# The last block's gate pieces leave on SyncE's queue instead of ScalarE's, spread over the end of one stage and the start of the next

## The chip, the cores and the metric

The kernel runs on one core of one Trainium2 chip, as one launch. The metric is device time in microseconds, the median of several executions.

## The reference

One inference step of a two-layer backbone over 384 tokens (128 of context, 256 latent). Each layer mixes tokens (short convolution, pooling, attention) and then mixes channels with a product-key expert retrieval over 16,384 experts. The change lies in that second half, which is by far the longer one:

```python
def _peer(x, w_q, sub_keys, u, v):          # D = 1024, 8 heads, 128 keys, top 16
    q = (xt @ w_q).reshape(T, PEER_HEADS, 2, PEER_HALF)
    s = jnp.einsum('thpd,hpkd->thpk', q, sub_keys)
    sv, si = lax.top_k(s, PEER_TOPK)
    cand = sv[:, :, 0, :, None] + sv[:, :, 1, None, :]
    top, f = lax.top_k(cand, PEER_TOPK)
    experts = i1 * PEER_KEYS + i2                      # i1, i2 looked up through f
    gates = jax.nn.softmax(top, axis=-1)
    h = jax.nn.gelu(jnp.einsum('tkd,td->tk', u[ec], xc))
    return jnp.einsum('tk,tkd->td', gc * h, v[ec])
```

## The kernel before

The kernel does not gather experts for most tokens. For 352 of the 384 tokens it computes the retrieval densely, in two stages per layer. The other 32 tokens (the "sparse" ones, the last of the third token block) go through gathered rows of `u` and `v`.

**The first stage** makes the hidden activations. It has 128 units, one for each block of 128 experts (`hidden_step`, L941 to L952 on TensorE). A unit is 24 matmuls: eight slices of `D`, and for each three products (`h_lo*u_hi`, `h_hi*u_hi`, `h_hi*u_lo`), since a 32-bit number is split in a high and a low part. ScalarE makes the high part of the weights (`u_hi`, L1229) and VectorE the low part (`u_lo`, L1642), both for the unit after next's buffer, so TensorE's unit 121 can't start before ScalarE and VectorE have treated its weights. ScalarE also applies the gelu to each finished unit (`act_h`, L1222, L1245) into a ring of four buffers, from which SyncE stores it to `act_scratch` in device memory (L510). Each gelu waits for the store of four units before.

**The gates.** Beside the first stage the routing of the three token blocks runs on VectorE. For a dense block the gates then have to be laid out over all experts: 16 gate steps scatter them into `g_all`, a tile of 128 keys x 128 tokens per partition. A block's `g_all` goes out to `gate_scratch` in eight pieces of 16 keys, 1024 KB each, in rows of 128 tokens (512 bytes). One semaphore for each piece (`g_st[0]` to `g_st[7]`) counts its landing. The two dense blocks are number 1 and 2 of the order. Block 1's pieces go out on SyncE's queue, one at a time between other things (`store_gates`, L495 to L499, called in L523). Block 2, the last, has its gates complete after unit 119 of the stage. Its eight pieces are issued by ScalarE in a row at L1291 to L1295, ahead of the gelu of unit 119 (`last_gelu`, L1245) and of the weights of unit 121. Eight units are left then: 120 to 127.

**The second stage** multiplies by `v`. It has 256 units of 12 matmuls (L1011), in groups of eight: a group is four blocks of 128 experts in two halves of the output. ScalarE and VectorE split the weights again (`v_hi` L1304, `v_lo` L1859; each instruction serves two units), and once per four units VectorE multiplies activation and gate (`w` from `act`, `gate`, L1868), with `w_hi` (L1311) and `w_lo` (L1872) behind it. Each of these engines works through one fixed order: in step 8(g-1) VectorE multiplies the first `w` of group g, and behind it in the row stands the `v_lo` of the pair of units 8(g-1)+2.

SyncE's queue brings in the data, each step waiting for the release of a buffer:

- `wring`, four slots of 1024 KB: `u` for the first stage, `v` for the second (`load_v`, L550), one slot per half group.
- `gate2` and `act2`, two buffers of a group each: `load_ga` (L543 to L547), 704 KB of gates and 704 KB of activations. Group 4 and later are loaded in a hardware loop (L592) that runs from group 4 to 31.
- Before the loop SyncE waits for all of `g_st[3:]` and `act_st` (L586 to L591).

GpSimd waits for every `g_st` and for the last unit of the first stage before it writes into the space of `g_all`: it makes `sel` (L712), then in the first layer loads `c_b` and `mod_w` (L719, L622; 1024 KB each) for the next layer's modulation, and in both layers fetches rows of `v` for the sparse tokens (L617). ScalarE needs `c_b` at step 22 of the second stage (L1339), VectorE the first two rows at step 24 (L1881).

Of the kernel before, what the change touches and what calls it, by code (L numbers as in the profile page):

```python
# [16 lines left out]
P = 128  # L17
# [5 lines left out]
TB = T // P  # L23
# [42 lines left out]
WR = 4  # L66
AR = 4
# [11 lines left out]
GT = TB - SCATTERED  # L79
# [3 lines left out]
ORDER = (2, 0, 1)  # L83
# [15 lines left out]
PIECES = 8  # L99
# [28 lines left out]
def build(nc, x_t, c_t, c_rows, vecs_t, w_ada, w_mod, w_in, w_out, w_q, subkeys_t, u_t, v_t, u_rows, v_rows, bias_t, pool_t, ck_t, cv_t, consts,  # L128
# [87 lines left out]
    g_all = at("g_all", [P, NK, P])  # L216
# [40 lines left out]
    gate_dram = nc.dram_tensor("gate_scratch", (NK, P, T), F32).ap()  # L257
# [7 lines left out]
    def S(name, per, credit=0):  # L265
        return Signal(nc, ctx, name, per, credit)
# [81 lines left out]
    tq_evac = S("tq_evac", NQ, credit=2)  # L348
    g_st = [S(f"g_st{i}", 16 * GT, credit=16) for i in range(PIECES)]
# [16 lines left out]
    sc_st = S("sc_st", 16 * PH * TOPK)  # L366

    uhi_rdy = S("uhi_rdy", NB)
    ulo_rdy = S("ulo_rdy", NB)
    h_mm = S("h_mm", NB, credit=2)  # L370
    gelu_rdy = S("gelu_rdy", NB, credit=2)
    act_st = [S(f"act_st{i}", 16 * (NB // AR), credit=16) for i in range(AR)]
# [27 lines left out]
    sp_passed = S("sp_passed", 0)  # L400
# [63 lines left out]
    def _(sp):  # L464
# [8 lines left out]
        for l in range(DEPTH):  # L473
# [31 lines left out]
            def store_acts(i, s):  # L505

                sp.wait_ge(gelu_rdy.sem, gelu_rdy.at(l, 0) + (i * (2 * WR) + 2 * (s - WR)))
                for b in range(2):
                    p = 2 * ((s + 1) % 2) + b
                    sp.dma_start(act_dram[i * (2 * WR) + (2 * (s - WR - 1) + b), :, 0:TD], act_h[:, p, 0:TD]) \  # L510
                      .then_inc(act_st[p].sem, 16)
# [22 lines left out]
            for turn in range(3, NB // 8):  # L534
                tb = max((b for b in range(SCATTERED, TB) if GATES_END[b] < turn), default=None)
# [7 lines left out]
            def load_ga(g, buf):  # L543

                for dst, src in ((gate2, gate_dram), (act2, act_dram)):
                    sp.dma_start(dst[:, buf, :, 0:TD], src[bass.ds(g * G, G), :, 0:TD].rearrange("b e t -> e b t")) \
                      .then_inc(ga_ld[buf].sem, 16)  # L547

            def load_v(g, half, slot):
                sp.dma_start(wring[:, slot].rearrange("p k n -> p (k n)"), v_t[l, g, half]).then_inc(w_ld[slot].sem, 16)  # L550

            for n in range(WR + 1):

                if n < WR:
                    sp.wait_ge(ulo_rdy.sem, ulo_rdy.at(l, NB + 2 * (n + 1 - WR)))
                    load_v(n // 2, n % 2, n)
                if n:
                    store_acts(NB // (2 * WR), n)
                if n == 1:
                    for sig in g_st[:2]:  # L560
                        sp.wait_ge(sig.sem, sig.at(l, 16 * GT))
                        sp.sem_inc(sp_passed.sem, 1)
                    for sig in act_st:
                        sp.wait_ge(sig.sem, sig.at(l, 16 * (4 * G // AR)))
                        sp.sem_inc(sp_passed.sem, 1)
                    sp.wait_ge(sc_st.sem, sc_st.at(l, 16 * PH * TOPK))
                    sp.sem_inc(sp_passed.sem, 1)
                    load_ga(0, 0)
                    sp.wait_ge(g_st[2].sem, g_st[2].at(l, 16 * GT))
                    sp.sem_inc(sp_passed.sem, 1)  # L570
                    load_ga(1, 1)
            def group_loads(g, n, ga=True):

                if ga:
                    sp.wait_ge(w32_rdy.sem, l * NB + (g - 1) * G)
                    load_ga(g, n)
                for half in range(2):
                    slot = 2 * n + half

                    sp.wait_ge(vlo_rdy.sem, l * NV + (g * (2 * G) + (G * (half - 3) + vlo_rdy.credit)))  # L580
                    load_v(g, half, slot)

            for n in range(2):
                group_loads(2 + n, n)
            for sig in g_st[3:]:
                sp.wait_ge(sig.sem, sig.at(l, 16 * GT))  # L586
                sp.sem_inc(sp_passed.sem, 1)
# [448 lines left out]
    def _(act):  # L1036
# [63 lines left out]
        for l in range(DEPTH):  # L1100
# [46 lines left out]
            for n in range(NU + 2):  # L1147
# [8 lines left out]
                if n < NU:  # L1156
                    keys = P if unit(n)[1] == 0 else KEYS
# [89 lines left out]
            for tb in range(TB):  # L1247
# [23 lines left out]
                for g in range(GATE_STEPS):  # L1271
# [5 lines left out]
                    for k in range(4):  # L1277
                        t = 8 * g + 4 + k
# [7 lines left out]
                                   ps[:, 0].rearrange("p (t i) -> p i t", t=4)).then_inc(gq_evac.sem, 1)  # L1286
                    act.wait_ge(tq_mm.sem, Q + (1 + tq_mm.credit))
                    nc.scalar.copy(g_all[:, :, 8 * g + 4:8 * g + 8], two_halves(g)[:, 0]).then_inc(half_rdy.sem, 1)
                if tb + 1 == TB:
                    act.wait_ge(tq_evac.sem, tq_evac.at(l, NQ))  # L1290
                    act.wait_ge(gq_evac.sem, gq_evac.at(l, NQ))  # L1291
                    for piece in range(PIECES):
                        keys = slice(piece * (NK // PIECES), (piece + 1) * (NK // PIECES))
                        act.dma_start(gate_dram[keys, :, ORDER[tb] * P:(ORDER[tb] + 1) * P].rearrange("a b t -> b a t"), g_all[:, keys]) \  # L1294
                            .then_inc(g_st[piece].sem, 16)  # L1295
                last_gelu(GATES_END[tb])
            def v_hi_step(i, n, lap=0):

# [735 lines left out]
```

## Time and profile before

| | |
|---|---|
| time, median of 3 runs | 2777.58 us (2775.84 to 2782.12) |
| the profiled execution | 2781.91 us, its span 2780.1 us |
| TensorE matmul busy | 2652.0 us, 95% of the span |
| VectorE | 1975.0 us, 71% |
| ScalarE | 1216.4 us, 44% |
| GpSimd | 681.6 us, 25% |
| chain that ended last | TensorE 77%, VectorE 11%, issue 4%, DMA 3%, ScalarE 2%, ScalarE's DMA issues 2% |
| DMA | 632.86 MB, 228 GB/s over the span |
| SyncE's queue (q1), ScalarE's queue (q10) | 500.51 MB and 16.78 MB |

The span is what the instructions cover; the execution's own time is 1.8 us more. TensorE is busy almost throughout, so what matters are the few places where it is not. "ACTq" and "SPq" are the two sequencers while they issue a DMA; such time doesn't count as busy. ScalarE's queue carries nothing but the sixteen pieces (eight in each layer).

### The profile page before, as it was taken

Reading aid. Unit: us, or ns where it says so; the run is one execution under the profiler, and the core shown is the slowest. Engines: PE = TensorE matmul, PEld = TensorE weight load, DVE = VectorE, ACT = ScalarE, POOL = GpSimd, SP = SyncE. Lnnn points to the kernel's source line nnn. Section 1 sums busy time; section 2 is a strip of 40 time slices with the busy share of each in tenths; the row PEclk is TensorE's granted clock in tenths of the full one; section 3 lists DMA queues with packets and bytes.
Section 4 is the critical chain, followed back from the end, with each engine's and each line's share of the span. In section 5 each row is a group of like instructions: output and inputs, shape, how many; then the busy total and the mean of one; then the engine's idle time right before and its main releaser. Section 6 shows DMA issues by size and latency. Waiting matters only on the chain.

```text
span 2780.1 us, 44944 instructions
## 1 busy us (share of the span) xinstructions
PE 2652.0 (95%) x16866; PEld 2592.2 (93%) x16866; DVE 1975.0 (71%) x3668; ACT 1216.4 (44%) x2061; POOL 681.6 (25%) x493
## 2 busy tenths in 40 slices
PE   7999999999996999999999899999999789999998
PEld 6979999899996999999998899998999789999998
DVE  3536686998893688888765567789988645666664
ACT  3444543366473433333354454334745533333333
POOL 0011008777600111111111000477764000101010
PEclk8999999999998999999999899999999999999999
DMA  7383359757948889898645124896596587777771
GB/s 299 125 313 132 132 190 347 224 154 191 257 132 268 322 312 345 315 341 324 245 155 159 61 107 168 293 280 179 143 259 188 173 285 280 257 277 266 268 265 73
DMA packets 274517, 632.86 MB, mean 228 GB/s; under 512 B 43888, under 2 KB 208112, under 8 KB 229296
## 3 DMA queue, kind: packets, MB, share of 16 engines
q1 hardware_dynamic: 185856, 500.51, 51.8%
q0 software_dynamic: 55472, 113.44, 13.4%
q10 hardware_dynamic: 33024, 16.78, 2.1%
q8 instruction: 95, 1.56, 0.2%
q14 instruction: 70, 0.57, 0.1%
HBM read 535.59 MB, written 94.99 MB: 227 GB/s over the span
## 4 chain that ended last, share of the span: by engine, by line
PE 77%; DVE 11%; issue 4%; DMA 3%; ACT 2%; ACTq 2%; POOL 1%; SPq 0%; POOLq 0%; DVEq 0%
PE ps L1011 33%; PE ps L952 23%; PE ps L806 11%; DVE u_lo L1642 3%; PE ps L828 2%; PE ps L976 2%; ACTq L1294 2%; DMA act_scratch<-act_h 2%; PE ps L913 1%; PE ps L982 1%; PE ps L935 1%; PE ps L902 1%; DVE u_rows_s L1654 1%; PE ps L881 1%; DVE best_iu L1734 1%
## 5 line engine op out<-in xcount | busy, mean ns | idle before, releaser
L952 PE MATMUL ps<-h_lo,u_hi 128*128 128x352 f32 x2048 | 668.6, 326 | 70.5 <-DVE u_lo L1642 69.4
L1011 PE MATMUL ps<-w_hi,v_lo 128*128 128x352 f32 (+1 forms) x2048 | 661.9, 323 | 5.3 <-DVE v_lo L1859 5.1
L1011 PE MATMUL ps<-w_hi,v_hi 128*128 128x352 f32 x2048 | 664.6, 324 | 0.0
L952 PE MATMUL ps<-h_hi,u_hi 128*128 128x352 f32 x2048 | 663.4, 324 | 0.0
L952 PE MATMUL ps<-h_hi,u_lo 128*128 128x352 f32 x2048 | 662.3, 323 | 0.0
L1011 PE MATMUL ps<-w_lo,v_hi 128*128 128x352 f32 x2048 | 659.7, 322 | 0.0
L1304 ACT CAST v_hi<-wring 128x1024 fp32r<-128x1024 f32 x256 | 268.5, 1049 | 607.8 <-PE ps L1011 607.8
L1859 DVE TENSOR_TENSOR v_lo<-wring,v_hi 128x1024 fp32r<-128x1024 f32 x256 | 313.4, 1224 | 282.5 <-ACT v_hi L1304 282.5
L703 POOL DMA_INDIRECT gate_scratch<-scat_g,scat_i x256 | 435.6, 1701 | 151.2 <-issue 105.4
L952 PEld LDWEIGHTS ps<-h_lo,u_hi 128*128 128x128 f32 x2048 | 386.6, 189 | 84.1 <-DVE u_lo L1642 82.7
L1642 DVE TENSOR_TENSOR u_lo<-wring,u_hi 128x1024 fp32r<-128x1024 f32 x256 | 312.7, 1222 | 202.7 <-ACT u_hi L1229 199.9
L1011 PEld LDWEIGHTS ps<-w_hi,v_lo 128*128 128x128 f32 x2048 | 383.9, 187 | 6.5 <-DVE v_lo L1859 6.5
L1011 PEld LDWEIGHTS ps<-w_lo,v_hi 128*128 128x128 f32 x2048 | 388.7, 190 | 0.0
L952 PEld LDWEIGHTS ps<-h_hi,u_lo 128*128 128x128 f32 x2048 | 387.4, 189 | 0.0
L952 PEld LDWEIGHTS ps<-h_hi,u_hi 128*128 128x128 f32 x2048 | 386.8, 189 | 0.0
L1011 PEld LDWEIGHTS ps<-w_hi,v_hi 128*128 128x128 f32 x2048 | 384.9, 188 | 0.0
L1222 ACT ACTIVATE act_h<-ps 128x352 f32<-128x352 f32 x250 | 117.2, 469 | 458.9 <-PE ps L952 404.9
L1229 ACT CAST u_hi<-wring 128x1024 fp32r<-128x1024 f32 x256 | 267.1, 1043 | 0.0
L617 POOL DMA_INDIRECT v_rows_s<-in_v_rows_dram,pick_s x64 | 88.0, 1375 | 556.2 <-PE ps L1011 546.1
L806 PE MATMUL ps<-g_lo,u_hi 128*128 128x386 f32 x576 | 198.6, 345 | 6.6 <-DVE g_lo L1417 5.6
L806 PE MATMUL ps<-g_hi,u_lo 128*128 128x386 f32 x576 | 196.3, 341 | 0.0
L806 PE MATMUL ps<-g_hi,u_hi 128*128 128x386 f32 x576 | 196.0, 340 | 0.0
(267 smaller groups left out, 3444.9 us busy)
## 6 DMA issues: line engine op xcount, KB each, us to landing
wring<-in_u_t_dram SPq DMA_DIRECT2D x128, 1024.0 KB, 5.6
wring<-in_v_t_dram SPq DMA_DIRECT2D x128, 1024.0 KB, 5.5
act_scratch<-act_h SPq DMA_DIRECT2D x256, 176.0 KB, 5.9
gate<-gate_scratch SPq DMA_DIRECT2D x64, 704.0 KB, 6.5
act<-act_scratch SPq DMA_DIRECT2D x64, 704.0 KB, 8.5
wring<-in_w_ada_dram SPq DMA_DIRECT2D x24, 1024.0 KB, 6.3
mod_w<-in_w_mod_dram POOLq DMA_DIRECT2D x24, 1024.0 KB, 7.4
wring<-in_w_in_dram SPq DMA_DIRECT2D x20, 1024.0 KB, 4.8
```

The costliest lines, as they stand in the source:

```text
L617: pool.indirect_dma_start(v_rows_s[:, s % V_RING], None, v_rows, bass.IndirectOffsetOnAxis(ap=pick_s[:, 0, s:s + 1].bitcast(U32), axis=0)) \
L703: pool.indirect_dma_start(gate_cells, bass.IndirectOffsetOnAxis(ap=scat_i[0:P - NS, j:j + 1], axis=0), scat_g[0:P - NS, j:j + 1], None, co ...
L806: last = nc.tensor.matmul(ps[:, bank, 0:TS], w[:, M % 2, k], gx[:, k, 0:TS], start=(k == 0 and n == 0), stop=(k == KC - 1 and n == 2))
L828: last = nc.tensor.matmul(ps[:, m % 2, 0:T], w[:, m % 2, k], hx[:, k, 0:T], start=(k == 0 and n == 0), stop=(k == KC - 1 and n == 2))
L952: last = nc.tensor.matmul(ps[:, 6 + s % 2, 0:TD], u[:, s % 2, k], hx[:, k, 0:TD], start=(k == 0 and n == 0), stop=(k == KC - 1 and n == 2))
L976: last = nc.tensor.matmul(ps[:, 0, k * P:(k + 1) * P], one_a[:, k], one_b[:, k], start=True, stop=True)
L1011: last = nc.tensor.matmul(ps[:, half * (KC // 2) + c, cols], v[:, of % 4, d], w[:, group * G + of, cols], start=(opening and k == 0), stop ...
L1222: nc.scalar.activation(act_h[:, p, 0:TD], ps[:, 6 + p % 2, 0:TD], ACT.Gelu_apprx_tanh) \
L1229: nc.scalar.copy(u_hi[:, b].rearrange("p k e -> p (k e)"), wring[:, slot].rearrange("p k n -> p (k n)")[:, b * D:(b + 1) * D]) \
L1304: nc.scalar.copy(v_hi[:, n % 4:n % 4 + 2].rearrange("p a n -> p (a n)"), wring[:, tile].rearrange("p k n -> p (k n)") [:, (n % G) * 512:(n ...
L1642: V.tensor_tensor(u_lo[:, b].rearrange("p k e -> p (k e)"), wring[:, slot].rearrange("p k n -> p (k n)")[:, b * D:(b + 1) * D], u_hi[:, b] ...
L1859: V.tensor_tensor(v_lo[:, n % 4:n % 4 + 2].rearrange("p a n -> p (a n)"), wring[:, n // G].rearrange("p k n -> p (k n)") [:, (n % G) * 512 ...
```

## The change

ScalarE's loop over the eight pieces of the last block goes, with its two waits. SyncE issues the pieces instead: piece 0 as soon as the gates are complete, pieces 1 and 2 each behind a load of `v` and two stores of activations, still in the first stage; pieces 3 and 4 behind the loads for group 2 and pieces 5, 6 and 7 behind those for group 3, in the second stage. The loop over `n` is written out as `first_v` calls, the two `load_ga` before the stage stand farther apart, and the waits ahead of them come in another order. The wait for `g_st[3:]` before the hardware loop and GpSimd's wait for all `g_st` stay as they are.

```diff
-            for n in range(WR + 1):
-                if n < WR:
-                    sp.wait_ge(ulo_rdy.sem, ulo_rdy.at(l, NB + 2 * (n + 1 - WR)))
-                    load_v(n // 2, n % 2, n)
-                if n:
-                    store_acts(NB // (2 * WR), n)
-                if n == 1:
...
-                    load_ga(0, 0)
-                    sp.wait_ge(g_st[2].sem, g_st[2].at(l, 16 * GT))
-                    sp.sem_inc(sp_passed.sem, 1)
-                    load_ga(1, 1)
+            def first_v(n):
+                sp.wait_ge(ulo_rdy.sem, ulo_rdy.at(l, NB + 2 * (n + 1 - WR)))
+                load_v(n // 2, n % 2, n)
+
+            gates_made(TB - 1)
+            store_gates(TB - 1, 0)
+            first_v(0)
+            store_acts(NB // (2 * WR), 1)
+            store_gates(TB - 1, 1)
+            first_v(1)
+            store_acts(NB // (2 * WR), 2)
+            store_gates(TB - 1, 2)
...
+            load_ga(0, 0)
+            first_v(2)
+            store_acts(NB // (2 * WR), 3)
+            sp.wait_ge(g_st[2].sem, g_st[2].at(l, 16 * GT))
+            sp.sem_inc(sp_passed.sem, 1)
+            load_ga(1, 1)
+            first_v(3)
+            store_acts(NB // (2 * WR), 4)
...
             for n in range(2):
                 group_loads(2 + n, n)
+                for piece in ((3, 4), (5, 6, 7))[n]:
+                    store_gates(TB - 1, piece)
             for sig in g_st[3:]:
                 sp.wait_ge(sig.sem, sig.at(l, 16 * GT))
...
-                if tb + 1 == TB:
-                    act.wait_ge(tq_evac.sem, tq_evac.at(l, NQ))
-                    act.wait_ge(gq_evac.sem, gq_evac.at(l, NQ))
-                    for piece in range(PIECES):
...
-                        act.dma_start(gate_dram[keys, :, ORDER[tb] * P:(ORDER[tb] + 1) * P].rearrange("a b t -> b a t"), g_all[:, keys]) \
-                            .then_inc(g_st[piece].sem, 16)
                 last_gelu(GATES_END[tb])
```

ScalarE's row at the end of the last gate step, first layer, before the change (line numbers of the kernel before):

```order
L1285 COPY g_all<-ps 128x128x4
L1288 COPY g_all<-ps 128x128x4
L1294 DMA gate_scratch<-g_all 128x16x128 x8
L1245 ACTIVATE act_h<-ps 128x352
L1229 CAST u_hi<-wring 128x1024
L1222 ACTIVATE act_h<-ps 128x352
```

And with the change, in which the same lines stand twelve lines lower:

```order
L1297 COPY g_all<-ps 128x128x4
L1300 COPY g_all<-ps 128x128x4
L1257 ACTIVATE act_h<-ps 128x352
L1241 CAST u_hi<-wring 128x1024
L1234 ACTIVATE act_h<-ps 128x352
```

The eight transfers are gone from the row, and the gelu of unit 119 follows the last copy directly.

SyncE's row from the last stores of the loop over `u` to the end of group 1's loads, first layer, before:

```order
L510 DMA act_scratch<-act_h 128x352 x4
L550 DMA wring<-in_v_t_dram 128x2048 x2
L510 DMA act_scratch<-act_h 128x352 x2
L546 DMA gate_120<-gate_scratch 128x4x352
L546 DMA act_121<-act_scratch 128x4x352
L546 DMA gate_120<-gate_scratch 128x4x352
L546 DMA act_121<-act_scratch 128x4x352
L550 DMA wring<-in_v_t_dram 128x2048
L510 DMA act_scratch<-act_h 128x352 x2
L550 DMA wring<-in_v_t_dram 128x2048
L510 DMA act_scratch<-act_h 128x352 x4
```

With the change, up to the load of group 1:

```order
L510 DMA act_scratch<-act_h 128x352 x4
L498 DMA gate_scratch<-g_all 128x16x128
L550 DMA wring<-in_v_t_dram 128x2048
L510 DMA act_scratch<-act_h 128x352 x2
L498 DMA gate_scratch<-g_all 128x16x128
L550 DMA wring<-in_v_t_dram 128x2048
L510 DMA act_scratch<-act_h 128x352 x2
L498 DMA gate_scratch<-g_all 128x16x128
L546 DMA gate_120<-gate_scratch 128x4x352
L546 DMA act_121<-act_scratch 128x4x352
L550 DMA wring<-in_v_t_dram 128x2048
L510 DMA act_scratch<-act_h 128x352 x2
```

Three pieces now stand between the loads of `v` and the stores, and group 1's pair comes behind the third load of `v`.

SyncE's row from group 2's loads to the branch into the hardware loop, with the change:

```order
L546 DMA gate_120<-gate_scratch 128x4x352
L546 DMA act_121<-act_scratch 128x4x352
L550 DMA wring<-in_v_t_dram 128x2048 x2
L498 DMA gate_scratch<-g_all 128x16x128 x2
L546 DMA gate_120<-gate_scratch 128x4x352
L546 DMA act_121<-act_scratch 128x4x352
L550 DMA wring<-in_v_t_dram 128x2048 x2
L498 DMA gate_scratch<-g_all 128x16x128 x3
L604 UNCONDITIONAL_BRANCH
```

Before, the same row held neither of the two L498 entries.

## Rows read from the trace of the kernel before

**Rows 1.** The waits, summed over the span: in total, times, longest.

```profile
DVE u_lo L1642 <- ACT u_hi L1229: 199.9, 97, 26.1
```

**Rows 2.** Chain that ended last, 780 to 1100 us: start, duration, what.

```profile
848.33 1.90 ACTq L1294
850.25 3.63 ACTq L1294
...
868.70 3.66 ACTq L1294
872.82 1.04 ACT u_hi L1229
```

**Rows 3.** Timeline of TensorE: start, duration, line, what, idle time before it.

```profile
850.00 0.32 PE L952 MATMUL ps<-h_hi,u_lo 128*128 128x352 f32 x1
875.17 0.66 PE L952 MATMUL ps<-h_lo,u_hi 128*128 128x352 f32 x1 [24.85 <-DVE u_lo L1642]
...
903.98 0.34 PE L1011 MATMUL ps<-w_hi,v_lo 128*128 128x384 f32 x1
...
2232.99 0.66 PE L952 MATMUL ps<-h_lo,u_hi 128*128 128x352 f32 x1 [24.80 <-DVE u_lo L1642]
```

**Rows 4.** Timeline of ScalarE after the pieces, first and second layer.

```profile
880.98 0.47 ACT L1222 ACTIVATE act_h<-ps 128x352 f32<-128x352 f32 x1 [5.82 <-PE ps L952]
...
884.84 0.47 ACT L1222 ACTIVATE act_h<-ps 128x352 f32<-128x352 f32 x1 [2.46 <-PE ps L952]
...
949.62 1.92 ACT L1339 ACTIVATE c_b<-c_b 128x2048 f32<-128x2048 f32 x1
...
2239.11 0.46 ACT L1222 ACTIVATE act_h<-ps 128x352 f32<-128x352 f32 x1 [6.13 <-PE ps L952]
```

**Rows 5.** Pieces by line, SyncE's then ScalarE's: issue in ns, landing in us.

```profile
L498 SPq DMA_DIRECT2D gate_scratch<-g_all x16: 382/383/383, 673.1 to 2101.8; - x16
DMA to landing us min/median/max: 6.0/6.8/8.1
...
DMA to landing us min/median/max: 5.2/10.3/13.7
```

**Rows 6.** Timeline of VectorE around the start of the second stage.

```profile
900.23 0.83 DVE L1868 TENSOR_TENSOR w<-act,gate 128x704 f32<-128x704 f32 x1
...
906.09 0.89 DVE L1868 TENSOR_TENSOR w<-act,gate 128x704 f32<-128x704 f32 x1 [0.24 <-DVE w_lo L1872]
906.90 1.22 DVE L1859 TENSOR_TENSOR v_lo<-wring,v_hi 128x1024 fp32r<-128x1024 f32 x1
...
920.93 0.89 DVE L1868 TENSOR_TENSOR w<-act,gate 128x704 f32<-128x704 f32 x1 [2.23 <-DMA act<-act_scratch]
```

**Rows 7.** Landing of L546's pairs issued at 884-889, 905-907 and 2289-2292 us.

```profile
DMA to landing us min/median/max: 6.5/8.6/10.5
...
DMA to landing us min/median/max: 12.8/13.5/14.3
...
DMA to landing us min/median/max: 6.7/8.2/9.6
```

**Rows 8.** Timeline of SyncE in the second stage: issues for groups 3 and 4.

```profile
915.21 0.45 SPq L546 DMA_DIRECT2D gate<-gate_scratch  x1
...
922.99 7.68 SPq L550 DMA_DIRECT2D wring<-in_v_t_dram  x2
931.70 0.40 SPq L546 DMA_DIRECT2D gate<-gate_scratch  x1
```

**Rows 9.** One stretch of the second stage: busy times, granted clock, DMA share, GB/s.

```profile
908.20:923.70 15.50, 15.50 (x96) 15.50 (x97) 8.76 (x9) 5.62 (x6) 0.00 (x0) 1.00 1.01 396
```

**Rows 10.** Timeline of GpSimd after the first stage, and the landing of its first load.

```profile
904.32 0.25 POOL L712 TENSOR_TENSOR sel<-cst 128x32 f32<-128x32 f32 x1 [143.87 <-PE ps L952]
...
905.90 0.62 POOL L719 DMA_DIRECT2D c_b<-in_c_rows_dram  x1
```

```profile
c_b<-in_c_rows_dram POOLq DMA_DIRECT2D x1, 1024.0 KB, 6.5
```

More of the change, by code:

```diff
@@ L550, in load_v @@
                 sp.dma_start(wring[:, slot].rearrange("p k n -> p (k n)"), v_t[l, g, half]).then_inc(w_ld[slot].sem, 16)
-            for n in range(WR + 1):
-                if n < WR:
-                    sp.wait_ge(ulo_rdy.sem, ulo_rdy.at(l, NB + 2 * (n + 1 - WR)))
-                    load_v(n // 2, n % 2, n)
-                if n:
-                    store_acts(NB // (2 * WR), n)
-                if n == 1:
-                    for sig in g_st[:2]:
-                        sp.wait_ge(sig.sem, sig.at(l, 16 * GT))
-                        sp.sem_inc(sp_passed.sem, 1)
[L563 to L567, printed above, removed]
-                    load_ga(0, 0)
-                    sp.wait_ge(g_st[2].sem, g_st[2].at(l, 16 * GT))
-                    sp.sem_inc(sp_passed.sem, 1)
-                    load_ga(1, 1)
+            def first_v(n):
[9 more added lines that the diff above has]
+            store_gates(TB - 1, 2)
+            for sig in act_st:
+                sp.wait_ge(sig.sem, sig.at(l, 16 * (4 * G // AR)))
+                sp.sem_inc(sp_passed.sem, 1)
+            sp.wait_ge(sc_st.sem, sc_st.at(l, 16 * PH * TOPK))
+            sp.sem_inc(sp_passed.sem, 1)
+            for sig in g_st[:2]:
+                sp.wait_ge(sig.sem, sig.at(l, 16 * GT))
+                sp.sem_inc(sp_passed.sem, 1)
+            load_ga(0, 0)
+            first_v(2)
+            store_acts(NB // (2 * WR), 3)
+            sp.wait_ge(g_st[2].sem, g_st[2].at(l, 16 * GT))
+            sp.sem_inc(sp_passed.sem, 1)
+            load_ga(1, 1)
+            first_v(3)
+            store_acts(NB // (2 * WR), 4)
             def group_loads(g, n, ga=True):
@@ L1288, in _ @@
                     nc.scalar.copy(g_all[:, :, 8 * g + 4:8 * g + 8], two_halves(g)[:, 0]).then_inc(half_rdy.sem, 1)
-                if tb + 1 == TB:
-                    act.wait_ge(tq_evac.sem, tq_evac.at(l, NQ))
-                    act.wait_ge(gq_evac.sem, gq_evac.at(l, NQ))
-                    for piece in range(PIECES):
-                        keys = slice(piece * (NK // PIECES), (piece + 1) * (NK // PIECES))
-                        act.dma_start(gate_dram[keys, :, ORDER[tb] * P:(ORDER[tb] + 1) * P].rearrange("a b t -> b a t"), g_all[:, keys]) \
-                            .then_inc(g_st[piece].sem, 16)
                 last_gelu(GATES_END[tb])
```

## The prediction

> **What bounds the kernel now.** I read the page first (TensorE is busy 95% of the span), then the waits. Their row to look at is that of `u_lo`, which waits for ScalarE 97 times with a longest of 26.1 us [rows 1], far out of line with a usual wait of a microsecond or two. The chain of waits around the longest one shows where it comes from: ScalarE's sequencer issues the eight gate pieces, the second in 1.90 us and each later one in about 3.66, and only then makes the `u_hi` of unit 121 at 872.82 [rows 2]. TensorE's timeline gives the price: its last matmul of unit 120 starts at 850.00, the first of unit 121 at 875.17, after 24.85 us of idleness; in the second layer it is 24.80 [rows 3]. So the pieces are on the path that sets the end, twice.
>
> There is a second, smaller price. Unit 121's first matmul lasts 0.66 us where the one before the stall lasts 0.32 [rows 3], and the whole unit is slow: its gelu starts at 880.98, 5.8 us after the unit's start, while the next comes 3.86 us later [rows 4]. That is 1.9 us; in the second layer 2239.11 less 2232.99 is 6.1 us, so 2.2 us [rows 3, 4].
>
> **What goes.** With the loop gone ScalarE passes from the last copy to the gelu of unit 119 and the weights of unit 121, which are ready before unit 120 ends at 850.3, as in all gate steps ahead of it. Gain: 24.85 + 1.9 + 24.80 + 2.2 = 53.8 us. Everything in the first stage's tail then stands 26.8 us earlier: the first matmul of the second stage, which I call S, moves from 903.98 [rows 3] to 877.2. Nothing of this gain needs the issue to be cheap on SyncE, only that nobody on the path waits for SyncE. That is the rest of the sum.
>
> **What an issue costs on SyncE.** Block 1's sixteen pieces, issued there with other things between, take 0.38 us each and land after 6.0 to 8.1 us; ScalarE's, in a row, land after 10.3 in the median [rows 5]. The first is the price of the issue, and 3.66 us is the rate at which 1024 KB of 512-byte rows drain, once two pieces are under way [rows 2]. Here the Trainium skill speaks against the change ("DMA: Bandwidth & Descriptors", section "Issuing engines are not separate DMA queues"): spreading DMAs over engines saves only the sequencer's time to initiate them, usually small beside the DMA. By that rule, with 0.38 us a piece, sixteen pieces would free some 6 us of ScalarE; the trace disagrees, since a piece held ScalarE for 3.66 us. But its other half, that all share the same sixteen engines, holds: the 3.66 us of draining go along to SyncE's queue.
>
> **The tail, 850 to 877.** Piece 0 goes out at about 849, piece 1 at 855.7 (behind the gelu of unit 121 and its stores), piece 2 at 863.3, each alone, so SyncE isn't held. Group 0's pair goes out right behind piece 2, at 863.8, since pieces 0 and 1 have landed. It drains behind piece 2 and should take the 10.5 us of [rows 7]: 874.3, against 900.23 - 26.8 = 873.4, when VectorE is ready for the first `w` [rows 6]. Group 1's pair must wait for piece 2 (863.3 + 6.8 or 10.3) and for the stores of units 124 and 125 at 870.1: it goes out at 871 to 873.6 and lands at 877.5 to 884, against 906.09 - 26.8 = 879.3 [rows 6]. Behind that `w` stands the `v_lo` of units 2 and 3; it ended at 908.12 and TensorE needed it at 903.98 + 3.87 = 907.85 [rows 3, 6], so there is no slack, and lateness is paid in full. Cost per layer 0 to 5 us; I take 1.8, nearest to a pair landing at 881. The stores of activations keep their place in time: a gelu needs the store of four units before, issued some 11 us earlier against a landing of about 6.
>
> **The start of the second stage.** The times count from S. A unit lasts 1.93 us (half of 3.86 us for half the matmuls). VectorE multiplies group g's first `w` in step 8(g-1) and must have made the `v_lo` behind it by unit 8(g-1)+2. That needs the pair landed by S + 15.46(g-1) + 3.87 - 0.82 - 1.22 = S + 15.46(g-1) + 1.8. (Group 2 before: limit S + 17.3 = 921.3, landed 920.93 [rows 6]: no harm.)
>
> Group 3's pair went out at S + 11.2 [rows 8]; now pieces 3 and 4 are ahead of it, and it drains from S + 20.9: load of `v` from 10.9 at 396 GB/s [rows 9], 2.7 us, then 2 x 3.66. Its 1.44 MB take 3.6 us more, landing by about S + 27; limit S + 32.7. No cost.
>
> Group 4 is the place to look at. Before, its pair went out at S + 27.7, limit S + 48.2. Now pieces 5 to 7 go out behind the second load of `v` for group 3, at S + 26.7 (922.99 + 7.68, [rows 8]), and SyncE then waits for them to land. The queue before them is empty at about S + 29.9 (the pair to 24.5, two loads of `v` 2.7 each); three pieces add 11.0: drained at 40.9, landed at 43.3. The loop takes 1.0 us to start (930.67 to 931.70 [rows 8]), so the pair goes out at S + 44.3, and lands 6.9 to 9.6 us later as in the quiet case: S + 51.2 to 53.9, 3.0 to 5.7 us past the limit [rows 7]. I take 4 us for the second layer.
>
> In the first layer GpSimd, too, waits for all pieces. It came to `sel` at 904.32 and to `c_b` 1.6 us later [rows 10]; now it does at S + 43.3 and 45.1, so its 3 MB for the modulation fall on the late pair. Before, that collision made group 2's pair land after 14.3 us [rows 7]: S + 58.6, a stall of 10.4. By ScalarE: `c_b` lands after 6.5 us [rows 10], S + 51.6, its silu takes 1.92 [rows 4], and `v_hi` and `v_lo` of unit 26 (1.05 and 1.22) end near S + 56 where TensorE needs them at S + 50.2: some 6 to 7 us. The two run side by side; I take 9 between them (5 to 14). GpSimd's rows for the sparse tokens are late by as much, and hidden in the same stall.
>
> The skill's page on DMA (section "Queues, rings and completion order") says that each engine takes turns between queue rows, but serves one row in order. In the old kernel a load of `v` could pass between ScalarE's pieces; now it stands behind them. My sums for groups 3 and 4 go by that; by taking turns group 3's pair would land 7.3 us sooner, and nothing else changes.
>
> **The sum.** -53.8 + 2 x 1.8 + 4 + 9 = -37.2 us. The profiled execution (span 2780.1, own time 2781.9) would take 2744.7. It is 4.3 us above the median of the runs, so the median comes to 2740.4. Loops and all later groups find their loads in time as before: after group 4 SyncE is again a group ahead.
>
> **The rivals.**
> *All of it arrives.* Stalls in the tail and at group 4 are absorbed (the pieces drain at more than 286 GB/s, the pair lands in 5 us). For it: pairs have landed in 6.7 us. Against it: GpSimd's loads can't move ahead of the pieces. Gain over 48 us, up to 53.8: 2724 to 2730. Chance 0.13.
> *Back-pressure in the tail.* The sum of the tail's traffic (3 pieces, 4 loads of `v`, 2 pairs, the stores) is 3 x 3.66 + 4 x 2.7 + 2 x 3.6 and some 5 for the stores, 34 us in 27. If the stores of activations fall behind it, the gelu waits for its buffer, and with it `u_hi`. A landing of 13.7 us as with the slowest piece [rows 5] instead of the 11 allowed costs 2.7 at each of two or three pairs of units, in each layer 5 to 8 us: 2750 to 2765 in all. Chance 0.13.
> *Slower.* The place is SyncE's wait for pieces 3 to 7 ahead of the hardware loop. If the three last ones don't share one drain but land 13.7 us each one after the other, it ends at S + 26.7 + 41.1 = 67.8, and group 4's pair lands at S + 83 (14.3 us), 35 us late in each layer: -53.8 + 3.6 + 70 = +20, 2797. It decides the sign once the wait ends later than about S + 60. For it: DMA share 1.01 in this stretch [rows 9]. Against it: eight pieces in a row landed after 10.3 us each while overlapping. Chance 0.03.
> *It does not do what it says.* TensorE's idleness stays, since unit 121 waited for something else that came at the same time. Against it: `u_hi` starts the moment ScalarE is free [rows 2]. Within 6 us of before: chance 0.02.
>
> **How the numbers follow.** The forecast has 0.69: its own range is -20 to -48, 2730 to 2757. Of the rivals' 0.31, the fast end and most of the back-pressure case should be inside: 2727 to 2760. About 0.2% (5.6 us) is what a measurement can tell from no change: faster 0.95, same 0.02, slower 0.03.
>
> **What would show it.** The issues of pieces at 0.38 us on SyncE, and no wait of `u_lo` over 7 us in the first stage. Unit 121 right behind unit 120. In the tail, `w` waiting for the pairs of group 0 or 1 by 1 to 3 us. In the second stage TensorE waits near S + 50 for `v_lo`, 4 us in the second layer and more than that in the first, with DMA or `c_b` behind it; groups 2, 3 and 5 without a wait. The prediction is wrong if the stall near S + 50 is missing or over 15 us, or if gelus wait for stores in the tail.

## The result, and the profile after

| | before | after |
|---|---|---|
| median | 2779.85 us (4 runs) | 2751.11 us (4 runs, 2745.57 to 2755.03) |
| ratio to before | | 0.9894, 95% interval 0.9869 to 0.9919 |
| the profiled execution | 2781.91 us | 2745.57 us (span 2743.7) |
| TensorE waits for `u_lo` in the first stage | 69.4 us | 19.7 us |
| TensorE waits for `v_lo` in the second stage | 5.1 us | 25.6 us |

The change makes the kernel 28.7 us faster by the medians; 37 were forecast, a little more than the 23 to 36 us that the interval allows. From part 5 of the page before, the two groups of matmuls that start a unit:

```profile
L952 PE MATMUL ps<-h_lo,u_hi 128*128 128x352 f32 x2048 | 668.6, 326 | 70.5 <-DVE u_lo L1642 69.4
L1011 PE MATMUL ps<-w_hi,v_lo 128*128 128x352 f32 (+1 forms) x2048 | 661.9, 323 | 5.3 <-DVE v_lo L1859 5.1
```

Parts 4 and 5 of the page after:

```profile
PE 77%; DVE 11%; DMA 5%; issue 4%; ACT 2%; SPq 1%; POOL 0%; POOLq 0%; ACTq 0%; DVEq 0%
...
L1023 PE MATMUL ps<-w_hi,v_lo 128*128 128x352 f32 (+1 forms) x2048 | 665.8, 325 | 26.6 <-DVE v_lo L1864 25.6
L964 PE MATMUL ps<-h_lo,u_hi 128*128 128x352 f32 x2048 | 666.3, 325 | 21.0 <-DVE u_lo L1647 19.7
```

ScalarE's issues have left the chain, DMA has grown in it, and the idle time before TensorE has moved from the stage of `u` to the stage of `v`. (Lines stand twelve or five lower than before: L1241 is the cast to `u_hi`, L1234 and L1257 the gelu, L1023 the second stage's matmul, L1864 `v_lo`, L1873 the product `w`.)

**The stop that was to go is gone.** Before, on ScalarE's timeline in the first layer, 25.35 us lay between the last copy (846.52) and the gelu of unit 119:

```profile
847.87 24.49 ACTq L1294 DMA_DIRECT2D gate_scratch<-g_all  x8
872.46 0.46 ACT L1245 ACTIVATE act_h<-ps 128x352 f32<-128x352 f32 x1 [25.35 <-issue]
```

After, the gelu of unit 119 and `u_hi` of unit 121 follow the last copy, and the gelus of units 120 and 121 come at the usual distance of 3.84 us:

```profile
846.67 0.48 ACT L1257 ACTIVATE act_h<-ps 128x352 f32<-128x352 f32 x1
847.02 1.05 ACT L1241 CAST u_hi<-wring 128x1024 fp32r<-128x1024 f32 x1
850.02 0.46 ACT L1234 ACTIVATE act_h<-ps 128x352 f32<-128x352 f32 x1 [1.95 <-PE ps L964]
850.38 1.03 ACT L1241 CAST u_hi<-wring 128x1024 fp32r<-128x1024 f32 x1
853.86 0.46 ACT L1234 ACTIVATE act_h<-ps 128x352 f32<-128x352 f32 x1 [2.44 <-PE ps L964]
```

**What came instead.** All stops of TensorE of over 0.25 us in this part of the program, from its timeline; the first four in the first layer, the last four in the second. They answer to [rows 3].

```profile
877.66 0.41 PE L1023 MATMUL ps<-w_hi,v_lo 128*128 128x384 f32 x1 [0.80 <-DVE w_lo L1877]
885.43 0.66 PE L1023 MATMUL ps<-w_hi,v_lo 128*128 128x352 f32 x1 [3.63 <-DVE v_lo L1864]
940.70 0.66 PE L1023 MATMUL ps<-w_hi,v_lo 128*128 128x352 f32 x1 [7.28 <-DVE v_lo L1864]
950.28 0.66 PE L1023 MATMUL ps<-w_hi,v_lo 128*128 128x352 f32 x1 [2.92 <-DVE v_lo L1864]
2220.68 0.41 PE L1023 MATMUL ps<-w_hi,v_lo 128*128 128x384 f32 x1 [0.28 <-DVE w_lo L1877]
2227.64 0.43 PE L1023 MATMUL ps<-w_hi,v_lo 128*128 128x352 f32 x1 [2.81 <-DVE v_lo L1864]
2275.98 0.42 PE L1023 MATMUL ps<-w_hi,v_lo 128*128 128x352 f32 x1 [1.65 <-DVE v_lo L1864]
2282.29 0.42 PE L1023 MATMUL ps<-w_hi,v_lo 128*128 128x352 f32 x1 [2.21 <-DVE v_lo L1864]
```

Timeline of VectorE and ScalarE in the first layer: what each of the stops waited for. They answer to [rows 6] and the silu of [rows 4].

```profile
883.35 0.89 DVE L1873 TENSOR_TENSOR w<-act,gate 128x704 f32<-128x704 f32 x1 [2.97 <-DMA act<-act_scratch]
...
935.42 0.89 DVE L1873 TENSOR_TENSOR w<-act,gate 128x704 f32<-128x704 f32 x1 [7.24 <-DMA act<-act_scratch]
...
939.35 1.23 DVE L1864 TENSOR_TENSOR v_lo<-wring,v_hi 128x1024 fp32r<-128x1024 f32 x1 [3.03 <-ACT v_hi L1309]
...
948.34 0.75 DVE L1886 TENSOR_SCALAR acc_s<-v_rows_s,w_s 128x1024 f32<-128x1024 f32 x1 [6.96 <-DMA v_rows_s<-in_v_rows_dram,pick_s]
...
936.40 1.91 ACT L1344 ACTIVATE c_b<-c_b 128x2048 f32<-128x2048 f32 x1 [8.25 <-DMA c_b<-in_c_rows_dram]
```

The first is group 1's pair, the second group 4's, the third (939.35) the `v_lo` of unit 26, the fourth the first row for the sparse tokens, the last `c_b`. Two of them meet at unit 26, and they don't end together. VectorE had its pair at 935.42, but then waited 3.03 us more for ScalarE, whose `v_hi` stood behind `c_b`. So `c_b` ended last: without its wait the stop of 7.28 us would have been some 4 us long (an estimate: `w` at 935.42, `v_lo` behind it, unit 26 at about 937.6 instead of 940.70).

In the second layer there is no `c_b`. There the pair ended the stop of 1.65 us, and the rows for the sparse tokens the one of 2.21 us, which stands at unit 28. VectorE's timeline:

```profile
2273.82 0.89 DVE L1873 TENSOR_TENSOR w<-act,gate 128x704 f32<-128x704 f32 x1 [4.73 <-DMA act<-act_scratch]
...
2280.35 0.76 DVE L1886 TENSOR_SCALAR acc_s<-v_rows_s,w_s 128x1024 f32<-128x1024 f32 x1 [3.70 <-DMA v_rows_s<-in_v_rows_dram,pick_s]
```

The timelines of SyncE and GpSimd in the first layer show who kept the transfers:

```profile
856.55 2.75 SPq L550 DMA_DIRECT2D wring<-in_v_t_dram  x1
...
863.88 2.54 SPq L546 DMA_DIRECT2D gate<-gate_scratch  x1
...
893.75 5.29 SPq L498 DMA_DIRECT2D gate_scratch<-g_all  x2
899.08 3.92 SPq L546 DMA_DIRECT2D gate<-gate_scratch  x1
...
909.26 9.33 SPq L498 DMA_DIRECT2D gate_scratch<-g_all  x3
925.35 0.40 SPq L546 DMA_DIRECT2D gate<-gate_scratch  x1
```

```profile
924.92 0.31 POOL L724 TENSOR_TENSOR sel<-cst 128x32 f32<-128x32 f32 x1 [164.83 <-DMA gate_scratch<-g_all]
...
926.25 0.63 POOL L731 DMA_DIRECT2D c_b<-in_c_rows_dram  x1 [0.36 <-issue]
```

The first two lines stand behind a single piece each (1 and 2), and SyncE was held 2.75 and 2.54 us there. The last three pieces held it for 9.33 us. Group 4's pair and GpSimd's loads were issued within a microsecond of each other once all had landed, 20 us later for GpSimd than in [rows 10], although the stage began 26 us earlier.

**The clock.** The granted clock of the stretches around the stop of 7.28 us (columns: stretch, busy times, granted clock, DMA share, GB/s):

```profile
936.40:940.70 4.30, 0.00 (x0) 0.00 (x1) 1.35 (x2) 4.30 (x4) 0.00 (x0) 0.50 1.01 421
940.70:946.30 5.60, 5.60 (x19) 5.60 (x20) 0.67 (x1) 0.17 (x1) 0.00 (x0) 0.50 1.01 404
```

At 0.50 the engine runs at 1.2 GHz instead of 2.4. Eighteen matmuls after this stop start 0.29 us apart instead of 0.16, nine after each of the two others that open with 0.66 us: 2.5 + 1.4 + 1.35 = 5.2 us. No slow stretch followed the stops of the second layer, which open with 0.41 to 0.43 us.

**The balance.** Gain by the forecast's rows 53.8 us. Loss in the first layer 0.80 + 3.63 + 7.28 + 2.92 + 5.2 = 19.9, in the second 0.28 + 2.81 + 1.65 + 2.21 = 7.0. That leaves 26.9 us, which is the difference of the medians (28.7) within its uncertainty (23 to 36). The profiled executions differ by 36.3 us, though, 9.4 more. 6.1 us of that arise between the first projection and the first unit of the second layer (276.1 us before, 270.0 after), where no instruction was changed; the other 3 are spread and not accounted for. The same 40 us of the attention part, before and then after:

```profile
1520.00:1560.00 40.00, 34.12 (x164) 26.21 (x164) 18.71 (x59) 19.21 (x58) 1.15 (x1) 0.79 0.10 31
```

```profile
1511.70:1551.70 40.00, 32.94 (x182) 26.00 (x181) 18.92 (x59) 20.94 (x63) 1.15 (x1) 0.91 0.08 25
```

The granted clock was 0.79 in one execution and 0.91 in the other, in a part in which TensorE waits often. So a single profiled time would have made the forecast look better than it was.

### The profile page after: what moved, and what is told of

It reads as the page before. It is cut to its first block, busy times and chain, and to the rows that moved or that the text cites. A ratio compares the mean times of both kernels' runs of the same rounds, so it can differ in the third digit from the quotient of the medians.

```text
span 2743.7 us, 44946 instructions
## 1 busy us (share of the span) xinstructions
PE 2644.2 (96%) x16866; PEld 2585.8 (94%) x16866; DVE 1977.0 (72%) x3668; ACT 1217.0 (44%) x2061; POOL 681.1 (25%) x493
## 4 chain that ended last, share of the span: by engine, by line
PE 77%; DVE 11%; DMA 5%; issue 4%; ACT 2%; SPq 1%; POOL 0%; POOLq 0%; ACTq 0%; DVEq 0%
PE ps L1023 31%; PE ps L964 25%; PE ps L818 11%; DVE u_lo L1647 3%; PE ps L840 2%; DMA act_scratch<-act_h 2%; PE ps L988 2%; DMA v_rows_s<-in_v_rows_dram,pick_s 1%; PE ps L925 1%; PE ps L994 1%; DMA act<-act_scratch 1%; PE ps L947 1%; PE ps L914 1%; DVE best_iu L1739 1%; DMA gate_scratch<-g_all 1%
## 5 line engine op out<-in xcount | busy, mean ns | idle before, releaser
L1023 PE MATMUL ps<-w_hi,v_lo 128*128 128x352 f32 (+1 forms) x2048 | 665.8, 325 | 26.6 <-DVE v_lo L1864 25.6
L964 PE MATMUL ps<-h_lo,u_hi 128*128 128x352 f32 x2048 | 666.3, 325 | 21.0 <-DVE u_lo L1647 19.7
L1023 PE MATMUL ps<-w_hi,v_hi 128*128 128x352 f32 x2048 | 664.3, 324 | 0.0
L1023 PE MATMUL ps<-w_lo,v_hi 128*128 128x352 f32 x2048 | 663.9, 324 | 0.0
L1864 DVE TENSOR_TENSOR v_lo<-wring,v_hi 128x1024 fp32r<-128x1024 f32 x256 | 313.6, 1225 | 276.1 <-ACT v_hi L1309 276.1
L715 POOL DMA_INDIRECT gate_scratch<-scat_g,scat_i x256 | 442.3, 1728 | 148.0 <-issue 105.0
L1023 PEld LDWEIGHTS ps<-w_hi,v_lo 128*128 128x128 f32 x2048 | 388.2, 190 | 29.5 <-DVE v_lo L1864 18.4
L1023 PEld LDWEIGHTS ps<-w_lo,v_hi 128*128 128x128 f32 x2048 | 388.3, 190 | 0.0
L1023 PEld LDWEIGHTS ps<-w_hi,v_hi 128*128 128x128 f32 x2048 | 388.2, 190 | 0.0
L1234 ACT ACTIVATE act_h<-ps 128x352 f32<-128x352 f32 x250 | 117.3, 469 | 455.1 <-PE ps L964 407.8
L1241 ACT CAST u_hi<-wring 128x1024 fp32r<-128x1024 f32 x256 | 267.1, 1043 | 0.0
```

The source lines that it names most:

```text
L715: pool.indirect_dma_start(gate_cells, bass.IndirectOffsetOnAxis(ap=scat_i[0:P - NS, j:j + 1], axis=0), scat_g[0:P - NS, j:j + 1], None, co ...
L964: last = nc.tensor.matmul(ps[:, 6 + s % 2, 0:TD], u[:, s % 2, k], hx[:, k, 0:TD], start=(k == 0 and n == 0), stop=(k == KC - 1 and n == 2))
L1023: last = nc.tensor.matmul(ps[:, half * (KC // 2) + c, cols], v[:, of % 4, d], w[:, group * G + of, cols], start=(opening and k == 0), stop ...
L1234: nc.scalar.activation(act_h[:, p, 0:TD], ps[:, 6 + p % 2, 0:TD], ACT.Gelu_apprx_tanh) \
L1241: nc.scalar.copy(u_hi[:, b].rearrange("p k e -> p (k e)"), wring[:, slot].rearrange("p k n -> p (k n)")[:, b * D:(b + 1) * D]) \
L1864: V.tensor_tensor(v_lo[:, n % 4:n % 4 + 2].rearrange("p a n -> p (a n)"), wring[:, n // G].rearrange("p k n -> p (k n)") [:, (n % G) * 512 ...
```

## The experiments

My theory: what limits a piece is not who issues it but its drain of 3.66 us; spread out, it frees the path. What the second stage then loses comes from two waits for all pieces, SyncE's ahead of its loop and GpSimd's ahead of everything it does. The rival: the DMA engines are full in this part, so waits only say where the loss shows. A second rival: the queue matters, because ScalarE also computes. The kernels ran in three groups, each with its own runs of the kernel before: experiments 1 to 4 (16 runs, 2778.3 us), 5 to 8 on another chip (11 runs, 2791.62), and the repeat of 8 with experiment 9 (9 runs, 2776.21). So they are compared by their ratio to the kernel before, and by the stops in their traces. The changed kernel's own ratio, 0.9894 (0.9869 to 0.9919), comes from the runs of the result.

**1. SyncE's wait behind groups 4 and 5.** These groups need only piece 1. The wait for the stored activations moves ahead of their loads.

```diff
+            for n in range(2):
+                group_loads(4 + n, n)
             for sig in g_st[3:]:
                 sp.wait_ge(sig.sem, sig.at(l, 16 * GT))
...
-            with sp.Fori(2, NG // 2) as i:
+            with sp.Fori(3, NG // 2) as i:
```

> Only SyncE's wait is changed: groups 4 and 5 are loaded before SyncE waits for pieces 3 to 7 (they need piece 1 alone). My theory: two waits for all pieces hold the start of the second stage, SyncE's (pair of group 4) and GpSimd's (c_b and the first rows of v). With SyncE's alone gone, VectorE no longer waits for group 4's pair (4.7 us in the second layer, 7.2 in the first), but in the first layer TensorE still stops for c_b at unit 26 (5 to 8 us) and in both for the rows at unit 28. So TensorE's stalls there fall by some 2 us in the second layer and by 0 to 2 in the first: 1 to 4 us faster than the changed kernel's 2751. Rival (bandwidth: the DMA engines are full until the pieces are through, waits or no waits): group 4's pair lands as late as before behind the pieces and the stalls stay as they are, within 1 us.

Measured: 0.9895 (0.9874 to 0.9916), 2751.5 us; no gain that shows. VectorE's wait for group 4's pair shrank from 7.24 to 1.02 us:

```profile
930.50 0.89 DVE L1875 TENSOR_TENSOR w<-act,gate 128x704 f32<-128x704 f32 x1 [1.02 <-DMA act<-act_scratch]
...
947.89 0.75 DVE L1888 TENSOR_SCALAR acc_s<-v_rows_s,w_s 128x1024 f32<-128x1024 f32 x1 [4.98 <-DMA v_rows_s<-in_v_rows_dram,pick_s]
```

But TensorE stopped 7.52 and 0.86 us for `c_b` and the rows in the first layer, and in the second 3.61 us for the rows alone, where it had stopped 1.65 + 2.21. The stops at units 26 and 28 fell from 10.2 to 8.4 us in the first layer and from 3.9 to 3.6 in the second. That is 2.1 us, inside my 1 to 4, and less than ratios with intervals of 0.2% can show. It could not be much: in the first layer `c_b` had ended last, and in the second the rows of `v` took over what the pair gave up.

**2. GpSimd's wait split.** `sel` after pieces 0 to 2, `c_b` after 3 and 4, the first rows at once, `mod_w` after 5 to 7: each as its space in `g_all` becomes free.

```diff
-            for sig in g_st:
+            for sig in g_st[:3]:
                 pool.wait_ge(sig.sem, sig.at(l, 16 * GT))
...
+                for sig in g_st[3:5]:
+                    pool.wait_ge(sig.sem, sig.at(l, 16 * GT))
                 pool.dma_start(c_b[:]...
+            load_rows(l, 0)
+            load_rows(l, 1)
+            if l == 0:
+                for sig in g_st[5:]:
+                    pool.wait_ge(sig.sem, sig.at(l, 16 * GT))
                 load_mod(0)
```

> Only GpSimd's wait is split: sel after pieces 0 to 2, c_b after 3 and 4, the first two rows of v then at once, mod_w after 5 to 7. My theory: c_b and the rows arrive before steps 22 and 24, so in the first layer the stop for the rows (2.9 us and 1.3 us of slow clock) goes, and the stop at unit 26 shrinks from 7.3 us to what group 4's pair alone costs, 2 to 5 us; in the second layer the 2.2 us stop goes. Together 8 to 12 us faster than the changed kernel's 2751. Rival (bandwidth): the 3 MB come earlier and delay groups 2 and 3 instead, as they did in the kernel before the pieces were moved; gain 0 to 3 us.

Measured: 0.9880 (0.9861 to 0.9899), 2747.12 us, some 4 us by the ratio instead of the 8 to 12 expected, and not clear of the changed kernel's interval. The silu no longer waits and the stops for the rows are gone in both layers. But in the first layer group 4's pair, still behind SyncE's wait, is later than ever:

```profile
945.22 0.89 DVE L1880 TENSOR_TENSOR w<-act,gate 128x704 f32<-128x704 f32 x1 [14.39 <-DMA act<-act_scratch]
```

TensorE stops 11.31 us for it. That the pair alone would cost 2 to 5 us was wrong. `c_b` and the rows now drained beside pieces 5 to 7: these held SyncE for 14.77 us instead of 9.33, and the pair went out at 933.43 instead of 925.35, together with `mod_w`.

**3. Both waits.**

> Both edits together. My theory: no stop of TensorE is left near units 26 and 28 of either layer; only those of the first stage's tail stay (0.8 + 3.6 us and 1.5 us of slow clock in the first layer, 0.3 + 2.8 in the second). First layer 14 us less, second 4 us less: 2733 (2729 to 2739). Rival (bandwidth): the stops move to another group between 2 and 5 and the gain is under 6 us, 2745 or more.

Measured: 0.9844 (0.9824 to 0.9864), 2736.19 us. Against the changed kernel's 0.9894 the edits alone gave -0.01% and 0.14%, neither clear of noise; together 0.50%, or 14 us, which is. Of the stops near units 26 and 28 one of 2.52 us is left, in the first layer:

```profile
931.25 0.89 DVE L1882 TENSOR_TENSOR w<-act,gate 128x704 f32<-128x704 f32 x1 [5.61 <-DMA act<-act_scratch]
```

No stop moved to another group, so the bandwidth rival falls for all but this rest. The bytes are the same; two waits for more than was needed had kept them from being asked for in time. The rest is the pair behind pieces 5 to 7, which held SyncE for 14.54 us here.

**4. All eight in a row on SyncE,** at the moment the gates are complete. The other calls of `store_gates` for this block go.

```diff
             gates_made(TB - 1)
-            store_gates(TB - 1, 0)
+            for piece in range(PIECES):
+                store_gates(TB - 1, piece)
             first_v(0)
```

> All eight pieces on SyncE in one row, right when the gates are complete; nothing in the second stage. My theory: the 3.66 us of drain per piece hold whichever sequencer issues them, so SyncE is held for about 24.5 us; the stores of units 120 and 121 go out near 873 instead of 854, and the gelu of unit 124 with the weights behind it waits for their landing, near 879 instead of 866. TensorE stops some 10 to 14 us in each layer's tail, slow clock behind it, group 0's pair comes after 885. No stop near units 26 and 28. Each layer keeps 8 to 14 of its 26.8 us: 2752 to 2764, median guess 2757. Rival (moving to a queue with no compute behind it is all that matters, issue 0.38 us each): no stop in the tail, 2727 to 2735.

Measured: 0.9960 (0.9946 to 0.9973), 2765.72 us, a little above the range. SyncE's timeline has the row of [rows 2] again, and ScalarE's the gelu that now waits for its buffer:

```profile
847.45 24.73 SPq L498 DMA_DIRECT2D gate_scratch<-g_all  x8
```

```profile
883.81 0.46 ACT L1231 ACTIVATE act_h<-ps 128x352 f32<-128x352 f32 x1 [21.59 <-DMA act_scratch<-act_h]
```

TensorE stops 18.05 and 17.37 us in the tails, behind the gelu of unit 124, instead of 24.8. The move to another queue by itself brings 0.4%; the spreading brings the rest. Expected were 10 to 14 us; the stores landed near 883, not 879, since a load of `v` stood ahead of them and took 3.61 us to issue.

**5. Spread, but on ScalarE's queue.** The pieces stand behind ScalarE's steps at about the times at which SyncE issues them in the changed kernel; SyncE issues none of them.

```diff
+                if s in (2, 4):
+                    act_gates(s // 2)
...
+                if at_ in (6, 14):
+                    for piece in ((3, 4) if at_ == 6 else (5, 6, 7)):
+                        act_gates(piece)
```

> The eight pieces stay on ScalarE's queue, but are spread as in the changed kernel: 0 behind the last copy, 1 and 2 behind the gelus of units 121 and 123, 3 and 4 behind step 6 and 5 to 7 behind step 14 of the second stage. My theory (the spacing frees the path, not the queue): no stop of 24.8 us in the first stage, unit 121 right behind unit 120. Since two queues take turns at the DMA engines, SyncE's pairs may land 1 to 3 us earlier than in the changed kernel, but the third of the last three pieces holds ScalarE for 4 to 6 us inside the second stage, which stops TensorE for 3 to 5 us a layer. The two waits for all pieces stay: 2745 to 2762, about 2753. Rival (ScalarE's queue is what costs): 2765 or more, with u_hi held behind single pieces.

Measured: 0.9894 (0.9866 to 0.9922), beside 0.9898 (0.9873 to 0.9922) of the changed kernel on the same chip. In the tail a piece costs ScalarE 0.38 to 0.46 us; in the second stage the groups of two and three held it, as its timeline shows, and TensorE stopped 1.05 and 2.39 us behind them:

```profile
858.26 0.38 ACTq L1249 DMA_DIRECT2D gate_scratch<-g_all  x1
...
895.61 6.09 ACTq L1249 DMA_DIRECT2D gate_scratch<-g_all  x2
912.38 7.37 ACTq L1249 DMA_DIRECT2D gate_scratch<-g_all  x3
```

In return group 4's pair went out 45.7 us after the stage's start instead of 47.7, and VectorE waited 4.06 us for it instead of 7.24 or 8.80. `c_b` still ended last, and TensorE stopped 4.07 and 4.15 us at units 26 and 28. All its stops sum to 14.4 us in the first layer and 4.8 in the second; in the two profiled runs of the changed kernel it was 14.6 both times, and 7.0 and 6.5. The second rival falls: with the same spacing the queue makes no difference that these runs can tell, though the stops lie in other places, and a difference of up to 0.3% would not show.

**6. The changed kernel again.**

> The changed kernel once more, on the same chip as the three others. Its first runs gave 2751 us and the profiled one 2746, whose attention part in the second layer ran at a higher granted clock. I expect 2751 (2747 to 2755), with the stops of TensorE again at units 2, 26 and 28 of the second stage in the first layer, 14 us in sum, and 6 to 7 us in the second.

Measured: 2763.67 us beside 2791.62 for the kernel before, ratio 0.9898 (0.9873 to 0.9922). The absolute time was missed, as the kernel before ran 12 us longer there too; the ratio and the stops came again: in the first layer 3.43, 8.29 and 2.91 us, 14.6 in sum, in the second 2.70 and 3.83. `c_b` ended last at unit 26 again, by 2.48 us. In the second layer the 3.83 us were the pair's alone.

**7. Piece 2 directly behind piece 1, on top of both split waits.**

```diff
             store_gates(TB - 1, 1)
+            store_gates(TB - 1, 2)
             first_v(1)
             store_acts(NB // (2 * WR), 2)
-            store_gates(TB - 1, 2)
```

> On top of both split waits, piece 2 goes out directly behind piece 1 in the first stage's tail. My theory: what is left of the loss in the tail is group 1's pair waiting for piece 2 to land and draining behind it. With piece 2 some 7 us earlier group 1's pair still waits in line for the stores of units 124 and 125, so it goes out at about the same time, but group 0's pair and the second load of v no longer share the drain with piece 2: w for group 0 not late, group 1's stop falls from 3 us to 1 to 2 us per layer. 2 to 5 us faster than with both waits split (2736). Rival (the tail is short of bandwidth, 34 us of drain in 27): the order changes nothing, within 1 us.

Measured: 0.9862 (0.9838 to 0.9886). The stop for group 1's pair went from 3.62 and 3.08 us to 2.45 and 2.34, with one of 0.45 us ahead. The 2 to 5 us expected did not show: the time can't tell it from experiment 3 (0.9844). The two pieces held SyncE for 4.14 us, and the load of `v` behind them for 3.44.

**8. The five pieces of the second stage spread too,** one behind each load of `v` (3; 4; 5; 6 and 7).

```diff
-                group_loads(2 + n, n)
-                for piece in ((3, 4), (5, 6, 7))[n]:
-                    store_gates(TB - 1, piece)
+                group_loads(2 + n, n, pieces=(((3,), (4,)), ((5,), (6, 7)))[n])
```

> As the kernel with piece 2 behind piece 1, and the five pieces of the second stage one behind each load of v (3; 4; 5; 6 and 7). My theory: no more than two pieces are ever in line, SyncE is held under 3 us at an issue, and the stop of 2.5 us that group 4's pair still causes in the first layer goes or halves: 1 to 3 us faster than the kernel before it. Rival (the engines are full in this stretch whatever the order): group 3's pair is late instead, within 1 us or slower.

Measured: 0.9826 (0.9802 to 0.9851). VectorE's wait for group 4's pair is 2.21 us instead of 5.75, and TensorE does not stop for it. The ratio is 0.36%, or 10 us, under that of experiment 7, where 1 to 3 us were expected; the intervals overlap, and one stop of 2.67 us is all that went from the timeline, so most of the 10 us is not shown to be the edit's. Run once more, beside the last experiment:

> The kernel that the other one is built on, once more on the same chip: 0.983 of the kernel before, with stops of 0.9 and 2.7 us at the start of the second stage in the first layer and 2.3 us in the second.

0.9848 (0.9831 to 0.9865), with stops of 3.33, 1.13 and 2.33 us. The middle one, at unit 34, had not been there the first time.

**9. Group 1's pair ahead of the third load of `v` and of the stores.**

```diff
             load_ga(0, 0)
+            sp.wait_ge(g_st[2].sem, g_st[2].at(l, 16 * GT))
+            sp.sem_inc(sp_passed.sem, 1)
+            load_ga(1, 1)
             first_v(2)
             store_acts(NB // (2 * WR), 3)
-            sp.wait_ge(g_st[2].sem, g_st[2].at(l, 16 * GT))
-            sp.sem_inc(sp_passed.sem, 1)
-            load_ga(1, 1)
             first_v(3)
```

> As the last kernel (both waits split, piece 2 behind piece 1, the others spread), and group 1's pair goes out directly behind group 0's, ahead of the third load of v and of the stores of units 124 and 125. My theory: the stop of 2.3 to 2.9 us at unit 2 of each second stage comes from this pair going out behind those stores; some 4 us earlier it lands in time, and the stop goes in both layers, with its slow clock: 5 to 7 us faster than the kernel it is built on. Group 0's pair is unchanged. Rival (the tail is short of bandwidth): the stop stays, or the later loads of v stop TensorE at unit 8 or 12; within 1.5 us.

Measured: 0.9827 (0.9806 to 0.9847), 2731.30 us beside 2734.35 of the kernel it is built on. The wait for this pair is gone from VectorE's timeline in both layers; TensorE's keeps a pause of 0.89 us in each:

```profile
883.10 0.43 PE L1032 MATMUL ps<-w_hi,v_lo 128*128 128x352 f32 x1 [0.89 <-DVE v_lo L1873]
```

That pause is what group 0's pair leaves: VectorE waits 1.49 and 1.29 us for it and does not catch up by unit 2. So the cause of the stop was the place of group 1's pair, and not the bandwidth of the tail, since the same bytes were moved. The edit moves it ahead of the load of `v` and of the stores at once, so which of the two had kept it is not told apart. A stop of 2.19 us at unit 26 was back, so some of the saving went elsewhere. Expected were 5 to 7 us; the medians differ by 3, less than the two intervals can part. This kernel has the lowest time of all, 1.7% under the kernel before and 0.7% under the changed one; by its ratio it stands level with experiment 8 (0.9826 and 0.9848).

## Why the prediction was right, and where it was not

- **What goes (-53.8 us): right.** Unit 121 runs right behind unit 120; no slow matmuls there.
- **The cost of an issue: half right.** A piece alone took SyncE 0.38 to 0.49 us, but what stood right behind it was held for 2.5 to 2.75 us; I had written that SyncE isn't held in the tail. I also had it free in the second stage; the pair of pieces held it 5.29 us and the three 9.33. It cost nothing there, since what stood behind them had slack, and the drain was counted anyway.
- **The tail (2 x 1.8 us): too low.** Measured 0.80 + 3.63 and 1.4 us of slow clock in the first layer, 3.1 us in the second. The mechanism, group 1's pair late by the full amount, was right: it landed at 883.35 where I had bounds of 877.5 to 884. It went out at 870.97, at the early end, and took some 12 us to land, longer than the 10.5 of [rows 7]. Experiment 9 puts the blame on its place behind the third load of `v` and the stores.
- **Group 3's pair at no cost, group 4's late: right, the 4 us of the second layer partly by luck.** From the true start of the second stage, taking off 5.0 us of stop and slow clock there, the pair went out at S + 42.7 (forecast 44.3). In the second layer the stops sum to 3.9 us against 4, but only 1.65 of them are the pair's; 2.21 are the rows of `v`, which I had at nothing there. In the other profiled run of this kernel the pair alone cost 3.83.
- **The first layer's collision (9 us): the mis-sized term.** It measured 7.28 + 2.92 us of stops and 3.9 us of slow clock, 14.1. Of my two ways to unit 26 the pair's was to be the worse, 10.4 us late; it came to some 4, since the pair landed at S + 52.7 in the same count and not at 58.6. The way over `c_b` and ScalarE, for which I had 6 to 7, set the 7.28. The 9 between them was close to it, but for a reason that did not hold. Two things were left out. I had the rows of `v` "hidden in the same stall"; the profile gives 948.34 for them, 18.7 us after the issue of the second at 929.6, behind the 3 MB that the same late wait released, and beside what SyncE then asked for. And I priced the slow clock where it goes away and not where new stops, of 2.92 us and more in this trace, bring it back.
- **Back-pressure in the tail:** did not occur; no gelu waited for a store there. Experiment 4 shows the mechanism real once eight pieces stand ahead of the stores.
- **The rule on issuing engines.** The Trainium skill ("DMA: Bandwidth & Descriptors", section "Issuing engines are not separate DMA queues") holds that spreading over engines saves only sequencer time. Experiments 4 and 5 agree more than I gave it credit for: 0.9960 for the move alone, and no difference between the queues with equal spacing. What it calls small was 24.5 to 24.7 us for eight pieces in a row.
- **The time:** 2740.4 forecast, 2751.11 measured, 8 us less gain. Two terms of the sum were short, by 5 us each: the 9 of the first layer's collision (14.1 measured) and the 3.6 of the two tails (8.9, of which 1.4 are slow clock). That the profiled execution came within 1 us of its forecast (2745.57 against 2744.7) is luck.

## What to carry to other kernels

In these runs a sequencer was held by the drain of what it had issued: 2.5 to 2.75 us right behind one large transfer of short rows, 3.66 us from the third in a row on. So look at what stands behind such a transfer, and at what the sequencer owes next. When transfers move later, list every wait for "all of them", on every engine, and narrow each to the piece whose data or space it needs: here two such waits, narrowed singly, gave nothing that the times could show, and together 14 us. Before that, find out which of several late transfers ends last. Price each new stop of a busy TensorE with the slow clock behind it.

## What the runs showed of the hardware

- The same DMA, 1024 KB in rows of 512 bytes, took its sequencer 0.38 us alone, on either queue. Eight in a row took 24.49 us on ScalarE's (kernel before) and 24.73 on SyncE's (experiment 4), about 3.66 us each from the third on.
- Stops of 2.92 and 3.63 us were followed by nine matmuls at 1.2 GHz each and one of 7.28 us by eighteen, while those of 1.65 to 2.81 us were followed by none in this trace. The border isn't sharp: in the other profiled run of the same kernel a stop of 2.70 us was followed by slow matmuls at once, and one of 3.43 us only 1 us after it.
- With 3 MB for the modulation on GpSimd's queue, and 1.4 MB each for groups 4 and 5 and 2 MB of `v` on SyncE's, all asked for within 4 us, the first two fetches of rows of `v` landed 18.2 to 18.7 us after their issue, against 7.2 to 8.3 us in the kernel before. They were the last in line on GpSimd's queue.
